# Layer 1 of a hybrid decoder step: output-gate slabs and sample states moved into the slots of the chunk recurrence, with half-width level products, a head norm by logarithm and grouped log gates

## The chip, the cores and the metric

The kernel runs on one core of one Trainium2 chip. The metric is the time of one execution on the device in microseconds; below, "PE" is TensorE's matmul stream, "PEld" its weight loads, "DVE" VectorE, "ACT" ScalarE, "POOL" GpSimd and "SP" the engine that issues most DMAs.

## The reference, cut to what matters

The kernel computes one inference step of two layers for 528 prompt rows and 8 x 4 sample rows. The change concerns only the mixer of layer 1, a gated linear attention with 4 heads (key width 128, value width 256):

```
q, k, v, g, gd = split_cols(h @ w_in, ODD_SIZES)
loga = log_sigmoid(gd @ wgu + bg) / 16                 # one gate per key column and row
for each chunk:                                        # scan, state S (128 x 256 per head)
    b = cumsum(loga)
    o = (q * exp(b)) @ S  +  tril(att(q, k, decay)) @ v
    S = exp(b_last) * S + (k * exp(b_last - b)).T @ v
on = rmsnorm(o, gn) * silu(g)                          # per head; the output gate g
y  = on @ w_out
```

The prompt starts from S = 0 and passes 16 meta rows and then 512 rows; each of the 8 samples starts from a state of its own and has 4 rows. The new states are outputs too.

## The kernel before, in words

Activations lie as [128 partitions of the feature, rows]; there are R = 560 rows, in two halves of 280. Every large product is done to nearly full precision with three matmuls (high x high, low x high, high x low part). A weight matrix is cut into slabs of 256 columns: a DMA brings a slab into one of two slots of RAW, ACT copies its high part (`hi`), POOL subtracts for the low part (`lo`), and PE runs two tiles of 128 columns, each 8 k-steps x 2 halves x 3 matmuls, by the helper `tile_rows` (line 1808). Tile 0 goes to PSUM banks 0 and 1, tile 1 to banks 2 and 3; ACT empties the first and DVE the second. The semaphores are `raw_in`, `hi_done`, `lo_done`, `slab_used`, `acc_done` and `acc_free`.

Each engine has one instruction list in program order, and the order is written out by hand. In layer 1 the stages follow one another so:

- **Projections.** The slabs of q, of the 16 gate columns (`gd`), of k (`ok`, two slabs). Between `gd` and `ok` come the log gates, head by head: two matmuls per half on PE (line 2253), then Abs, Exp and Ln on ACT (lines 1146 to 1150), a min and a subtract on DVE (lines 1624, 1627). Then DVE runs the cumulative sum as four scans (line 1631), and after them empties its tiles of k (line 1616).
- **Levels.** The decayed attention inside a chunk of 64 rows is built from six levels (block sizes 64 to 2) and the diagonal, for two pairs of heads. For each level DVE makes exponents (1656, 1657), ACT exponentiates them, DVE and POOL scale queries and keys (1667, 830), PE makes 18 or 20 products of 64 x 64 (line 2290), and DVE copies the wanted quadrant of each block by a mask into ATT (1677). A product has all 64 query columns although only the later half of each block is kept. The four slabs of v (`ov`) and the first of the four output-gate slabs (`og`) are placed among them.
- **Chunk recurrence.** Rows are padded to 9 prompt chunks of 64 and one of the 32 sample rows. For each chunk PE transposes values and keys (2303, 2306), ACT copies them into VR and KR (1193, 1195), PE makes the state update (2340) and then 16 output products in two parts, from the state (2322) and from ATT (2324), and DVE forms the new state (1745) and moves the outputs into G (1731).
- **Samples.** For each of the 8 samples a DMA brings its state into SIN (512 KB, two buffers), PE makes its state update (2356) and the inter-part of its output (2361: 8 products with the state as weight and 4 moving columns), DVE forms the new state (1585), and a DMA stores it.
- **Head norm.** ACT squares, PE sums over the head's width with a matrix of ones (2373), ACT takes Sqrt (1200), DVE the reciprocal (1764).
- **Gate slabs 1 to 3** of `og` (their loads stand behind the samples in SP's list), Silu on ACT, two multiplies per tile on DVE (1772, 1778), the high and low parts (1226, 1781), and then the four slabs of `out1`, the first of which starts as its k-steps become ready.

Layer 1's feed-forward part and the final norm follow; they are not touched.

Of the kernel before, what the change touches and what calls it, by code (L numbers as in the profile page):

```python
# [23 lines left out]
ALU = mybir.AluOpType  # L24
# [185 lines left out]
def trunk(nc, t, o):  # L210
# [4 lines left out]
    with ExitStack() as ctx:  # L215
# [139 lines left out]
        GATE0 = LK[:, :, :, :].rearrange("p s h n -> p (s h n)")[:, 0:2 * R].rearrange("p (a n) -> p a n", a=2)  # L355
        LE = NRM[:, :, :].rearrange("p a n -> p (a n)")[:, 0:4 * GW].rearrange("p (s h n) -> p s h n", s=2, h=2)
        GSC = NRM[:, 0:2, :]
        GRR = NRM[:, 2:6, :]
        YR, _, _ = region("YR", [RB, 4, 512], F32, 0)
# [68 lines left out]
        WP = NCP * CH  # L428

# [85 lines left out]
        def _(sp):  # L515
# [30 lines left out]
            def load_pair(g, i):  # L546
# [17 lines left out]
                for j in range(2):  # L564
                    sp.wait_ge(lo_done, a + 2 * i + j - 1)
                    sp.dma_start(RAW[:, (a + j) % 2, 0:g.kcs[j], :], srcs[j]).then_inc(raw_in[(a + j) % 2], 16)
# [46 lines left out]
            load_pair(gemms["og"], 0)  # L613

            sgla = t["state_gla"][0]
            for b in range(DB):
# [13 lines left out]
            load_pair(gemms["og"], 1)  # L630
            for name in ("out1", "up1a", "down1a", "up1b", "down1b"):
# [212 lines left out]
        def _(act):  # L844
# [295 lines left out]

            for h in range(GH):
                L = GSC[:, h % 2, :]
                act.wait_ge(la_mm, h + 1)
                if h >= 2:
                    act.wait_ge(la_sub, h - 1)
# [3 lines left out]
                act.wait_ge(la_act, 2 * h + 1)  # L1149
                act.activation(L, L, ACT.Ln, bias=1.0).then_inc(la_act, 1)  # L1150
            odd_rows(gemms["ok"], 4)
# [30 lines left out]
            for j in range(2):  # L1182
                act.wait_ge(*tile_done(og, j, 0, 0))
                act.activation(halved(GATE0[:, j, :]), halves(j), ACT.Silu).then_inc(acc_free[j], 1)
            hi(og.slab0 + 1)

            for c in range(NCH):
                m = CH if c < NCP else NS
                act.wait_ge(vk_tr, c + 1)
                if c >= 2:  # L1190
                    act.wait_ge(o_done, c - 1)
                for par in range(2):
                    act.activation(VR[64 * par:64 * par + m, c % 2, :], PS[0:m, par, :], ACT.Copy)
                for par in range(2):
                    ins = act.activation(KR[64 * par:64 * par + m, c % 2, :], PS[0:m, 2, 2 * GDK * par:2 * GDK * par + 2 * GDK], ACT.Copy)
                ins.then_inc(vk_ev, 1)
# [1262 lines left out]
```

## Time and profile before

| what | value |
|---|---|
| median of 3 runs | 1714.29 us (1706.51 to 1719.15) |
| profiled execution, its own time | 1713.52 us |
| its span, first to last instruction | 1711.7 us |
| mean granted TensorE clock in it | 0.92 of full speed |
| PE busy | 1589.3 us, 93% of the span |
| DVE, ACT, POOL busy | 32%, 31%, 32% |

The rows below come from that one execution; its times count from the start of the span. A merged row of a timeline gives the start, the time from its first start to its last end, the count of instructions (xN), and in brackets how long the engine was idle before it and what ended that. An fp32 matmul stands in the trace as two instructions. "PEclk" is the granted clock, in shares of 2.4 GHz.

### The profile page before, as it was taken

What the parts mean: (1) busy time and instruction counts of PE and PEld (TensorE: products, weight loads), DVE (VectorE), ACT (ScalarE), POOL (GpSimd) and SP (SyncE); (2) the same over time, 40 slices, a digit from 0 to 9 for tenths busy, and PEclk for the clock granted to TensorE, in tenths of its full rate; (3) what the DMA queues carried; (4) which work ended last, traced back from release to release, by engine and by line L of the source; (5) the groups of instructions that cost most, each with busy time, mean ns of one, the idle gap of its engine ahead of it and who ended that gap; (6) DMA issues with size and microseconds to landing.
All of it is one profiled execution on the core that took longest, in us unless ns stands there. A gap on an engine that the chain in (4) does not pass through costs nothing.

```text
span 1711.7 us, 28133 instructions
## 1 busy us (share of the span) xinstructions
PE 1589.3 (93%) x11895; PEld 1479.4 (86%) x11895; DVE 550.5 (32%) x1005; ACT 534.5 (31%) x708; POOL 549.0 (32%) x203
## 2 busy tenths in 40 slices
PE   6888988988999999999888889999989999999996
PEld 5677756578999999999888887788989999999996
DVE  5168785533111101101317762236340111001113
ACT  4233443432433222223353231103333432222231
POOL 4322352022433434333345430002334343434240
PEclk8889996898999999999889897658989999999998
DMA  5531342002222232222222100044212222232221
GB/s 131 174 113 61 125 151 97 1 26 74 74 87 78 74 104 87 85 70 79 64 74 74 51 26 1 1 151 131 76 50 86 86 67 91 87 98 74 71 77 53
DMA packets 117076, 136.12 MB, mean 80 GB/s; under 512 B 5960, under 2 KB 111834, under 8 KB 114945
## 3 DMA queue, kind: packets, MB, share of 16 engines
q1 hardware_dynamic: 113189, 114.04, 21.5%
q0 software_dynamic: 3456, 20.97, 3.5%
q8 instruction: 56, 0.92, 0.2%
q14 instruction: 19, 0.16, 0.0%
q10 hardware_dynamic: 356, 0.03, 0.0%
HBM read 127.14 MB, written 7.94 MB: 79 GB/s over the span
## 4 chain that ended last, share of the span: by engine, by line
PE 87%; DVE 5%; ACT 4%; issue 2%; DMA 1%; POOL 0%; SPq 0%; DVEq 0%; ACTq 0%; POOLq 0%
PE PS L1808 67%; PE PS L2324 2%; PE PS L2361 2%; PE PS L2322 2%; PE PS L2143 1%; PE PS L2356 1%; PE PS L2037 1%; PE PS L2340 1%; PE PS L2290 1%; PE PS L2068 1%; PE PS L2128 1%; PE PS L2106 1%; PE PS L1836 1%; PE PS L2303 1%; PE PS L2025 1%
## 5 line engine op out<-in xcount | busy, mean ns | idle before, releaser
L1808 PE MATMUL PS<-HHI,WHI 128*128 128x280 f32 x2304 | 648.8, 299 | 22.0 <-DVE HLO L1270 10.8
L1808 PE MATMUL PS<-HLO,WHI 128*128 128x280 f32 x2304 | 641.8, 295 | 0.0
L670 POOL TENSOR_TENSOR WLO<-RAW,WHI 128x2048 fp32r<-128x2048 f32 (+2 forms) x89 | 366.1, 4114 | 855.2 <-ACT WHI L868 659.7
L1808 PE MATMUL PS<-HHI,WLO 128*128 128x280 f32 x2304 | 489.9, 295 | 0.0
L1808 PEld LDWEIGHTS PS<-HHI,WHI 128*128 128x128 f32 x2304 | 443.9, 193 | 33.6 <-issue 23.7
L1808 PEld LDWEIGHTS PS<-HLO,WHI 128*128 128x128 f32 x2304 | 443.4, 192 | 0.0
L1808 PEld LDWEIGHTS PS<-HHI,WLO 128*128 128x128 f32 x2304 | 373.2, 192 | 0.0
L868 ACT ACTIVATE WHI<-RAW 128x2048 fp32r<-128x2048 f32 x87 | 166.1, 1909 | 148.7 <-PE PS L1808 146.0
L1808 PE MATMUL PS<-ALO,WHI 128*128 128x280 f32 x704 | 192.8, 291 | 0.0
L1808 PE MATMUL PS<-AHI,WHI 128*128 128x280 f32 x704 | 192.8, 291 | 0.0
L1596 DVE TENSOR_TENSOR AT<-PS,SG 128x560 f32<-128x560 f32 x44 | 32.6, 742 | 473.4 <-PE PS L1808 473.4
L1808 PE MATMUL PS<-AHI,WLO 128*128 128x280 f32 x704 | 147.5, 291 | 0.0
L1569 DVE TENSOR_TENSOR XT<-PS,XT 128x560 f32 x48 | 35.6, 742 | 306.8 <-PE PS L1808 306.8
L1808 PEld LDWEIGHTS PS<-AHI,WHI 128*128 128x128 f32 x704 | 132.5, 188 | 0.0
L1808 PEld LDWEIGHTS PS<-ALO,WHI 128*128 128x128 f32 x704 | 132.3, 188 | 0.0
L1808 PEld LDWEIGHTS PS<-AHI,WLO 128*128 128x128 f32 x704 | 111.7, 188 | 0.0
L664 POOL TENSOR_TENSOR WLO<-RAW,WHI 128x2048 fp32r<-128x2048 f32 x16 | 76.1, 4755 | 99.9 <-ACT WHI L861 93.5
L1117 ACT ACTIVATE AHI<-AT 128x560 f32 x44 | 29.6, 673 | 224.5 <-DVE AT L1596 224.5
L1112 ACT ACTIVATE SG<-PS 128x560 f32<-128x560 f32 x44 | 28.1, 639 | 147.6 <-PE PS L1808 147.2
L893 ACT ACTIVATE NRM<-XT 128x560 f32 (+1 forms) x32 | 21.5, 672 | 135.0 <-DVE XT L1569 134.9
L861 ACT ACTIVATE WHI<-RAW 128x2048 fp32r<-128x2048 f32 x18 | 34.4, 1910 | 20.2 <-PE PS L1808 20.2
L692 POOL TENSOR_TENSOR HLO<-NRM,HHI 128x560 fp32r<-128x560 f32 x16 | 22.7, 1419 | 51.1 <-ACT HHI L886 51.1
(301 smaller groups left out, 1661.9 us busy)
## 6 DMA issues: line engine op xcount, KB each, us to landing
RAW<-in_ffn_w_gate SPq DMA_DIRECT2D x22, 1024.0 KB, 5.3
RAW<-in_ffn_w_up SPq DMA_DIRECT2D x22, 1024.0 KB, 5.3
RAW<-in_ffn_w_down SPq DMA_DIRECT2D x16, 768.0 KB, 4.5
RAW<-in_w_in_odd SPq DMA_DIRECT2D x12, 1024.0 KB, 5.3
RAW<-in_ffn_w_down SPq DMA_DIRECT2D x16, 640.0 KB, 4.3
RAW<-in_w_in_even SPq DMA_DIRECT2D x7, 1024.0 KB, 6.9
RAW<-in_w_out_even SPq DMA_DIRECT2D x4, 1024.0 KB, 5.2
SIN<-in_state_gla SPq DMA_DIRECT2D x8, 512.0 KB, 4.0
```

The lines of the kernel that those rows point to most:

```text
L664: pool.tensor_tensor(WLO[:, s % 2, 0:kc, :], RAW[:, s % 2, 0:kc, :], WHI[:, s % 2, 0:kc, :].bitcast(F32), ALU.subtract).then_inc(lo_done, 1)
L670: pool.tensor_tensor(WLO[:, par, 0:kc, :], RAW[:, par, 0:kc, :], WHI[:, par, 0:kc, :].bitcast(F32), ALU.subtract).then_inc(lo_done, 1)
L861: act.activation(WHI[:, s % 2, :, :], RAW[:, s % 2, :, :], ACT.Copy).then_inc(hi_done, 1)
L868: act.activation(WHI[:, s % 2, :, :], RAW[:, s % 2, :, :], ACT.Copy).then_inc(hi_done, 1)
L1112: act.activation(halved(SG[:, j, :]), halves(j), ACT.Silu).then_inc(acc_free[j], 1)
L1117: act.activation(AHI[:, ds(2 * i + j, 1), :].rearrange("p a n -> p (a n)"), AT[:, j, :], ACT.Copy).then_inc(ahi_ready, 1)
L1569: dve.tensor_tensor(x, halves(j), x, ALU.add).then_inc(acc_free[j], 1)
L1596: dve.tensor_tensor(halved(AT[:, j, :]), halves(j), halved(SG[:, j, :]), ALU.mult).then_inc(acc_free[j], 1)
L1808: ins = pe.matmul(acc[a][:, half, 0:HALF], w[:, slot, k, c0:c0 + P], x[:, k0 + k, HALF * half:HALF * half + HALF], start=first and n == 0 ...
L2322: pe.matmul(out, STATE[:, c % 2, h, 128 * e:128 * e + 128], G[:, h, CH * c:CH * c + m], start=True, stop=False)
L2324: ins = pe.matmul(out, VR[rows, c % 2, x:x + 128], ATT[rows, h // 2, CH * c:CH * c + m], start=not inter, stop=True)
L2361: ins = pe.matmul(PS[:, 7, y:y + DT], SIN[:, b % 2, h, 128 * e:128 * e + 128], G[:, h, WP + DT * b:WP + DT * b + DT], start=True, stop=True)
```

## The change

- **Log gates grouped.** ACT first copies the high part of slab `ok` 1, then does Abs and Exp for all four heads and after that Ln for all four, each head with a buffer of its own (LA). PE puts the first tile of `ok` between heads 1 and 2, and the second after head 3. DVE does the four min operations, then the four subtracts, then the scans.
- **Half-width levels.** The products of the six levels take only the later query half of each block, 32 columns of a chunk; the masked copy moves half as many elements.
- **Recurrence.** The chunk of the sample rows comes first (`CHUNKS`), with buffers of its own (VRS, KRS). The transposes of values and keys are separate steps in banks 2 and 3. The outputs go to banks 4 and 5, state updates of prompt and samples to banks 6 and 7. Gate slabs 1 to 3 are cut into 18 pieces (3, 3 and 2 k-steps of a tile), all in banks 0 and 1, two to a chunk. From the second chunk on, each chunk also does one sample: its update, and its output with the 32 masked query columns as weight (`QM`) and the state's 256 columns as moving operand, the four heads at four output partitions; DVE adds these up in OI, which PE turns back at the end. SP's list has the loads of `og` slabs 2 and 3 and of `out1` slab 0 moved ahead of, or among, the sample states. ACT applies Silu to each gate tile as it ends, into eight buffers in LK and BC.
- **Head norm.** Sqrt and reciprocal become Ln on ACT and Exp with scale -0.5 on ACT; the multiplies and low parts on DVE are interleaved by head; the gate slabs that stood behind the norm are gone from there.

The core of the diff (the buffers' definitions, the semaphore counts of loads and of two unchanged helpers are left out):

```diff
+        CHUNKS = [NCP] + list(range(NCP))
+        GATE_ENDS = [3 * x + 2 for x in range(6)]
@@ sync
+            load_pair(gemms["og"], 1, (0,))
             for b in range(DB):
...
+                if b == 1:
+                    load_pair(gemms["og"], 1, (1,))
+                if b in (4, 6):
+                    load_pair(gemms["out1"], 0, (b // 2 - 2,))
...
-            load_pair(gemms["og"], 1)
@@ scalar
+            hi(ok.slab0 + 1)
             for h in range(GH):
-                L = GSC[:, h % 2, :]
+                L = LA[:, h, :]
...
-                act.wait_ge(la_act, 2 * h + 1)
-                act.activation(L, L, ACT.Ln, bias=1.0).then_inc(la_act, 1)
+            for h in range(GH):
+                act.wait_ge(la_act, h + 1)
+                act.activation(LA[:, h, :], LA[:, h, :], ACT.Ln, bias=1.0).then_inc(la_act, 1)
...
+            for k in range(2):
+                values_out(k)
+                keys_out(k)
+            hi(og.slab0 + 2)
+            for c in range(NCP):
+                if c + 1 < NCP:
+                    values_out(c + 2)
+                gate_out(2 * c)
+                if c + 1 < NCP:
+                    keys_out(c + 2)
+                gate_out(2 * c + 1)
...
-                act.activation(halved(GRR[:, h, :]), ..., ACT.Sqrt, bias=CA[:, C_EPS:C_EPS + 1]).then_inc(ort, 1)
+                act.activation(halved(GRR[:, h, :]), ..., ACT.Ln, bias=CA[:, C_EPS:C_EPS + 1]).then_inc(ort, 1)
+            for h in range(GH):
+                act.wait_ge(ort, h + 1)
+                act.activation(GRR[:, h, :], GRR[:, h, :], ACT.Exp, scale=-0.5).then_inc(orr, 1)
@@ vector
+                ins = dve.copy_predicated(ATT[:, hp, 0:WP].rearrange("p (c b x) -> p c b x", c=NCP, x=size)[:, :, :, half:size],
+                                          late.unsqueeze(1).to_broadcast([P, NCP, CH // size, half]),
+                                          ps[:, 0:WP // 2].rearrange("p (c b x) -> p c b x", c=NCP, x=half))
...
+            for c in range(NCP):
+                if c:
+                    own_keys(c - 1)
+                new_state(c)
+                chunk_out(c)
+                if c:
+                    sample_out(c - 1)        # OI add, then new_states(b)
...
-                dve.reciprocal(GRR[:, h, :], GRR[:, h, :]).then_inc(orr, 1)
...
+                if h:
+                    gated_lo(2 * h - 2)
+                    gated_lo(2 * h - 1)
+            gated_lo(6)
+            gated_lo(7)
@@ tensor
+            for x in range(4):
+                log_gates(x)
+                if x % 2:
+                    one_tile(gemms["ok"], 0, x // 2)
+            for j in range(2):
+                one_tile(gemms["ok"], 1, j)
...
+            def state_update(c):
+                pe.wait_ge(vk_ev, 2 * c + 4)
+                if c:
+                    pe.wait_ge(s_new, GH * c)
+                if c >= 2:
+                    pe.wait_ge(sn_ready, GH * (c - 1))
...
+            def sample_products(b):
+                pe.wait_ge(st_in[b % 2], 16 * (b // 2 + 1))
+                pe.wait_ge(kb_ready, b + 1)
+                pe.wait_ge(s_new, GH * (b + 2))
+                ...                          # 4 updates into banks 6, 7
+                for h in range(GH):
+                    ins = pe.matmul(PS[NS * h:NS * h + NS, 3, 0:GDV], masked_query(h, b), SIN[:, b % 2, h, :], start=True, stop=True)
+                ins.then_inc(oi_done, 1)
...
+            for k in range(2):
+                value_turns(k)
+                key_turns(k)
+            chunk_products(NCP)
             for c in range(NCP):
+                state_update(c)
+                if c + 1 < NCP:
+                    value_turns(c + 2)
+                gate_piece(2 * c)
+                if c + 1 < NCP:
+                    key_turns(c + 2)
+                chunk_products(c)
+                if c:
+                    sample_products(c - 1)
+                gate_piece(2 * c + 1)
...
-            for n in range(1, 4):
-                one_slab(gemms["og"], n)
             slab_loop(gemms["out1"], [(o2lo, k + 1) for k in range(KC)])
```

## Rows read from the trace of the kernel before

**Rows 1.** The page, part 1: busy time, share of the span and instructions of each engine.

```profile
PE 1589.3 (93%) x11895; PEld 1479.4 (86%) x11895; DVE 550.5 (32%) x1005; ACT 534.5 (31%) x708; POOL 549.0 (32%) x203
```

**Rows 2.** Busy time by stretch: length, PE, PEld, DVE, ACT, POOL, PEclk, DMA share, GB/s.

```profile
878.80:921.90 43.10, 35.10 (x208) 31.62 (x208) 21.26 (x15) 24.45 (x26) 10.74 (x3) 0.84 0.24 74
921.90:1019.50 97.60, 87.13 (x1008) 84.85 (x1008) 74.46 (x74) 32.02 (x31) 41.54 (x16) 0.91 0.13 40
1019.50:1115.40 95.90, 91.88 (x464) 72.31 (x464) 21.57 (x55) 20.92 (x41) 4.51 (x1) 0.73 0.01 5
1115.40:1161.40 46.00, 45.89 (x208) 39.17 (x208) 15.70 (x42) 0.00 (x0) 0.00 (x0) 0.50 0.49 156
1161.40:1174.10 12.70, 9.92 (x34) 7.12 (x35) 5.31 (x3) 8.27 (x12) 0.00 (x0) 0.83 0.72 224
1174.10:1211.10 37.00, 37.00 (x288) 36.77 (x287) 24.33 (x18) 10.63 (x10) 14.40 (x3) 1.00 0.27 86
1211.10:1227.80 16.70, 14.12 (x96) 13.95 (x97) 7.39 (x13) 6.92 (x10) 4.61 (x1) 0.90 0.20 64
```

**Rows 3.** PE's timeline through chunk 1.

```profile
1027.74 1.13 PE L2340 MATMUL PS<-VR,KR 64*128 64x256 f32 x8 [0.97 <-ACT KR L1195]
...
1028.81 1.06 PE L2303 MATMUL PS<-CA,G 128*64 128x128 f32 x8
...
1030.14 0.33 PE L2322 MATMUL PS<-G,STATE 128*128 128x64 f32 x2
...
1035.50 0.48 PE L2340 MATMUL PS<-VR,KR 64*128 64x256 f32 x1
```

**Rows 4.** Busy time in chunk 1 and in a later chunk; columns as in rows 2.

```profile
1027.74:1035.50 7.76, 7.76 (x51) 6.37 (x52) 1.66 (x4) 1.93 (x4) 0.00 (x0) 1.00 0.00 0
1067.64:1081.72 14.08, 14.08 (x55) 11.05 (x55) 2.41 (x6) 1.93 (x4) 0.00 (x0) 0.50 0.00 0
```

**Rows 5.** The chain that ended last: start, us, what; recurrence, samples, norm.

```profile
1067.64 2.03 PE PS L2340 x8
...
1081.72 2.03 PE PS L2340 x8
...
1115.44 1.92 PE PS L2324 x16
1117.36 1.87 PE PS L2356 x8
...
1169.88 4.22 PE PS L2373 x16
```

**Rows 6.** Groups of ACT's instructions from 879 to 900 us: count, busy, mean ns.

```profile
L1148 ACT ACT_TABLE_LOAD x4 | 5.1, 1283 | 0.1
...
L1148 ACT ACTIVATE NRM<-NRM 128x560 f32<-128x560 f32 x4 | 2.7, 670 | 0.0
...
L868 ACT ACTIVATE WHI<-RAW 128x2048 fp32r<-128x2048 f32 x1 | 1.9, 1901 | 0.0
```

**Rows 7.** DVE's scans (minimum, median, longest ns), and its timeline after them.

```profile
L1631 DVE TENSOR_TENSOR_SCAN BC<-CG,BC x4: 1392/3564/5723, 899.9 to 912.5; 128x608 f32<-128x608 f32 x4
...
913.84 0.71 DVE L1616 TENSOR_SCALAR G<-PS 128x560 f32<-128x560 f32 x1
```

**Rows 8.** POOL's timeline around the scans.

```profile
901.03 4.65 POOL L670 TENSOR_TENSOR WLO<-RAW,WHI 128x2048 fp32r<-128x2048 f32 x1 [21.78 <-ACT WHI L868]
905.64 5.68 POOL L664 TENSOR_TENSOR WLO<-RAW,WHI 128x2048 fp32r<-128x2048 f32 x1
```

**Rows 9.** Groups by shape in the levels' stretch, from 919 to 1020 us.

```profile
L2290 PE MATMUL PS<-LQ,LK 128*64 128x64 f32 x432 | 16.4, 239 | 9.7 <-DVE LQ L1667 9.7
...
L1677 DVE COPY_PREDICATED ATT<-CG,PS 128x576 f32<-128x576 int32 x14 | 11.5, 821 | 17.0 <-PE PS L2290 16.8
```

**Rows 10.** The group of DVE's new sample states, four to a sample.

```profile
L1585 DVE SCALAR_TENSOR_TENSOR SNEW<-SIN,EB,PS 128x256 f32<-128x256 f32 x32 | 13.2, 476 | 26.6 <-PE PS L2356 26.6
```

**Rows 11.** The group of DVE's low parts behind the gates.

```profile
L1781 DVE TENSOR_TENSOR HLO<-G,HHI 128x560 fp32r<-128x560 f32 x8 | 5.3, 734 | 0.0
```

More of the change, by code:

```diff
@@ L563, in load_pair @@
                     srcs = [w[:, :, ds(c0 + 512 * i, 256)], w[:, :, ds(c0 + 512 * i + 256, 256)]]
-                for j in range(2):
+                for j in which:
                     sp.wait_ge(lo_done, a + 2 * i + j - 1)
@@ L629, in _ @@
             store(o["new_gla_prompt"][0, 0].rearrange("h d e -> d h e"), STATE[:, NCP % 2, :, :])
[L630 to L631 removed]
+            load_pair(gemms["out1"], 1)
+            for name in ("up1a", "down1a", "up1b", "down1b"):
                 load_all(gemms[name])
@@ L1183, in _, with values_out @@
                 act.wait_ge(*tile_done(og, j, 0, 0))
-                act.activation(halved(GATE0[:, j, :]), halves(j), ACT.Silu).then_inc(acc_free[j], 1)
+                act.activation(halved(gate(j)), halves(j), ACT.Silu).then_inc(acc_free[j], 1)
             hi(og.slab0 + 1)
-            for c in range(NCH):
+            def values_out(k):
+                c = CHUNKS[k]
                 m = CH if c < NCP else NS
[L1189 to L1196, printed above, removed]
+                act.wait_ge(vk_tr, 2 * k + 1)
+                if 2 <= c < NCP:
+                    act.wait_ge(o_done, c)
+                dst = VR[:, c % 2, :] if c < NCP else VRS
+                act.activation(dst[0:m, :], PS[0:m, 2, :], ACT.Copy)
+                act.activation(dst[64:64 + m, :], PS[0:m, 3, :], ACT.Copy).then_inc(vk_ev, 1)
@@ new lines, in keys_out, with gate_out @@
+            def keys_out(k):
+                c = CHUNKS[k]
+                m = CH if c < NCP else NS
+                act.wait_ge(vk_tr, 2 * k + 2)
+                dst = KR[:, c % 2, :] if c < NCP else KRS
+                act.activation(dst[0:m, :], PS[0:m, 2, 0:2 * GDK], ACT.Copy)
+                act.activation(dst[64:64 + m, :], PS[0:m, 2, 2 * GDK:4 * GDK], ACT.Copy).then_inc(vk_ev, 1)
+            def gate_out(piece):
+                if piece not in GATE_ENDS:
+                    return
+                x = GATE_ENDS.index(piece)
+                n, j = 1 + x // 2, x % 2
+                act.wait_ge(*tile_done(og, j, n, n))
+                act.activation(halved(gate(2 * n + j)), halves(0), ACT.Silu).then_inc(acc_free[j], 1)
+                if j and n < 3:
+                    hi(og.slab0 + n + 2)
@@ L2248, in _, with log_gates @@
             pe.wait_ge(ht_ready, KC * (norm_no["mix1"] + 1))
-            for h in range(GH):
+            def log_gates(h):
                 if h >= 2:
@@ L2364, in _ @@
+            pe.wait_ge(oi_ev, DB)
+            for e in range(2):
+                ins = pe.transpose(PS[:, 3, P * e:P * e + P], OI[:, P * e:P * e + P], ident(P))
+            ins.then_inc(oi_done, 1)
+            pe.wait_ge(s_new, GH * NCP)
+            pe.wait_ge(o_ev, NCH)
             pe.wait_ge(in_gla, 32)
@@ L2374, in _ @@
                     ins.then_inc(osq_used, 1)
-            for n in range(1, 4):
-                one_slab(gemms["og"], n)
             slab_loop(gemms["out1"], [(o2lo, k + 1) for k in range(KC)])
```

209 lines of the change are left out of this document (124 added, 85 removed).

## The prediction

> **What bounds the kernel now.** I read the page first, then busy time by stretch, then PE's own timeline inside the stretches that the change rebuilds. PE is busy for 93% of the span and the other three engines for about 32% each [rows 1]; so the question for every microsecond is whether PE does less, gets a higher clock, or stops waiting. The stretches [rows 2] answer it differently. In the log gates PE works 35.1 of 43.1 us: there is idle time. In the levels it works 87.1 of 97.6. In the recurrence (95.9 us), and still more in the samples (46.0 us, PE 45.9), PE is hardly ever idle, but its granted clock is 0.73 and 0.50. The three gate slabs (37.0 us) run at 1.00. So moving the gate slabs into the recurrence fills no holes: there are none. What it can win is cheaper sample products, clock, and the waits around the stretches.
>
> That the recurrence is slow by its clock is seen in two chunks. Chunk 1 takes 1035.50 - 1027.74 = 7.76 us at clock 1.00: update 1.07, twelve transposes 1.33, output products 5.36 (differences of starts) [rows 3, 4]. A later one takes 14.08 us at 0.50, its update 2.03 [rows 4, 5]. Chunks 1 to 8 together, from 1027.74 to 1115.44, take 87.7 us, 10.96 each: 3.2 us a chunk are lost to the clock.
>
> **Log gates.** Before, ACT loads a table ahead of every Exp and every Ln, 8 times 1.28 us (the four of one line are shown [rows 6]), and the scans start at 899.9. A scan takes 1.39 us undisturbed and up to 5.72 [rows 7]; the long ones lie beside POOL's two low parts, 901.0 to 911.3 [rows 8]. Only at 913.84 does DVE empty the k tile for which PE stands. After: six loads fewer (7.7 us), but heads 2 and 3 wait for PE's first k tile (37.0 / 6 = 6.2 us [rows 2]), so the subtracts end near 896, about 4 us earlier. The copy of slab `ok` 1 now stands ahead of the gates on ACT (1.9 us [rows 6], of which 0.6 delays the chain), so POOL's first low part comes before the scans and one is left beside them. Four scans: 4 x 1.4 plus one block of 4.6 gives 906.5, the evacuation 907.2, against 914.5: 7 us. If both blocks stay: 4; if none: 11. I take **-7**.
>
> **Levels.** The trace shows no 32-column product. The 432 records of 64 columns take 16.4 us of merged busy time [rows 9]. If the weight load sets the pace, half the columns bring nothing; if the columns do, 8 us. The masked copy (0.82 us; 12 of 14 halved) moves half the elements: at most 0.4 us each, 5 in all, but DVE lies on PE's path only where PE waits for it, 9.7 us in all [rows 9]. I take 2 + 2 = **-4**, between 0 and -11.
>
> **Recurrence with samples and gate pieces.** The old cost is 95.9 + 46.0 + 37.0 = 178.9 us [rows 2]. The new one, first at full clock:
> - Up to the end of chunk 0. Before, from 1019.5 to 1027.74 [rows 2, 3], 8.2 us: two sets of transposes with ACT's copies between them, an update, chunk 0's products. After: a third set, between 1.3 (transposes alone) and 4.1 (half of the 8.2), 2.5 taken; the sample chunk's products, 1.92 at half clock [rows 5], 1.0; two gate pieces, 2 x 37.0 / 18 = 4.1. Sum 15.8.
> - Chunks 1 to 8: 7.76 + 4.1 + one sample. The sample's update is the old one, 1.87 us at half clock [rows 5], about 1.0 at full. Its output product is new: eight instructions of 256 columns. One after the other, at the 0.264 us of a 280-column fp32 instruction (4.22 / 16 [rows 5]), they take 1.9; if the four heads, which fall on different output partitions, run fully side by side, 0.5. The levels' products, which lie on two partition halves, are the nearest: 16.4 / 432 = 0.04 us each [rows 9], where 64 of 280 columns at 0.264 would be 0.06, so they do overlap; I take 0.8. So 13.7 a chunk; eight make 109.6, less 1.3 because the last has no transposes: 108.3.
> - New waits on PE: `state_update` waits for the new sample states (`sn_ready`), since both use banks 6 and 7. Behind it stand the next transposes, a piece and all products, and ACT waits for those. DVE needs 4 x 0.476 [rows 10] and an add, some 2.3 us, after the sample's product; the piece between covers 2.3 us when it has 3 k-steps and 1.5 when it has 2. In all 2.5 us. `key_turns` waits for ACT's copy of values; all copies of a chunk are 1.93 us [rows 4], and a piece covers that share of it. Without that cover it would cost up to 1.9 a chunk.
> - Clock: I keep the 3.2 us a chunk of before, 25.6 in all. The output products, in which the clock was lost, are unchanged and now followed by a sample, which loses it too; the pieces bring it back, as `og` 1 to 3 hold 1.00, but each must first run part of itself slow. The bounds are 0 and the all-slow case below.
>
> Sum: 15.8 + 108.3 + 2.5 + 25.6 = 152.2, against 178.9: **-26.7**.
>
> Moved DMAs: SP issues the third gate slab ahead of the first sample state, the fourth after sample 0, and `out1` slab 0 among samples 3 to 6. Each is needed a chunk or more (some 17 us) after its issue, and the DMA share is 0.01 in the recurrence and 0.49 in the samples [rows 2], so I cost them at nothing; sample states are loaded two chunks ahead. POOL's low parts of four slabs now fall into the recurrence. The slowed scans show what one does to a DVE instruction beside it: up to 4.3 us [rows 7, 8]. DVE's steps in a chunk (2.41 us before [rows 4]) are done one chunk before PE needs them, so I take no loss; where one is hit with no cover, it costs those 4.3.
>
> **Tail.** Before, the norm stretch (12.7) and the start of `out1` (16.7) make 29.4 us [rows 2]; the reciprocals and most multiplies lay under the gate slabs. That cover is gone. After: turning OI and adding it, 1.2 (estimate); squares, sums and Ln in place of Sqrt as before, 12.5; Exp's table and one Exp, 1.28 + 0.67 [rows 6]; then 16 multiplies and 8 low parts on DVE at 5.3 / 8 = 0.66 us [rows 11], 15.9, with `out1`'s first slab behind them; PE ends some 4.2 later, its last three k-steps at 1.5. Sum 35.8: **+6.4**, from +4 to +11 (POOL's next low part can block one of DVE's).
>
> Total -7 - 4 - 26.7 + 6.4 = -31.3. The profiled execution took 1713.5 us, 0.8 below the median; that gives 1682, and I predict **1683 us** for the median.
>
> **A rule against the rows.** In the samples PE is busy 45.9 of 46.0 us, and its granted clock is 0.50 [rows 2]; a busy row doesn't bring the higher level here. The Trainium skill (TensorE: Matmul & The Clock Gate, Part 1: The HAM clock gate) tells it otherwise: a busy PE gets the full clock, and only an idle one falls back. By that rule the new recurrence, which has almost no idle time, would lose nothing, and the sum would be 1657; by the rows it is 1683. This trace disagrees with the rule as far as small products go.
>
> **Rivals.**
> - *Full clock.* The pieces, 18 wide matmuls or 12 each and twice a chunk, hold the clock at 1.00 through the products. Then the 25.6 us go: 1657. For it: chunk 1, soon after a gate slab, ran at 1.00 throughout [rows 4]. Against: the later chunk stayed at 0.50 although its update and transposes came between two sets of products. The rule above is this case. 0.15.
> - *Hand-overs.* The order is one chain now, PE to ACT to PE and PE to DVE to PE in each chunk, and one slab copy on ACT (1.9 us) or low part on POOL shifts it. With 2.2 us of waits a chunk instead of 0.3, and a blocked low part in the tail: 1683 + 15 + 5 = 1703. For it: banks 2, 3, 6 and 7 each change hands between prompt and sample work in every chunk. Against: in the old recurrence, with such a chain too, PE is busy 91.9 of 95.9 us [rows 2]. 0.22.
> - *Slower: the clock stays at half through the whole recurrence.* Then a chunk costs 14.08 + 7.8 (pieces, at the ratio 14.08 / 7.76 or a little more) + 3.5 (sample) = 25.4 instead of 13.7 + 3.2: 68 us more in eight, 1751. It decides from a loss of 7.1 us a chunk, where the whole gain is gone (9.2 for over 1% slower). For it: the samples never came back from 0.50. Against: in the old recurrence transposes and updates alone, 2.4 us of a chunk, brought the mean to 0.73. 0.07.
> - *The change doesn't do what it says in the small parts:* half-width products bring 0 and grouped gates 4 us: 1690, inside the forecast.
>
> **How the numbers follow.** My forecast, with a clock loss between 2 and 4.5 us a chunk and the bounds above, reaches from 1671 to 1696 and has 0.56. The range for 8 in 10 takes in much of the full-clock case and of the hand-overs: 1660 to 1704. A change under 1% (17 us; the three runs spread over 0.7%) can't well be told from none. Faster by more than that, below 1697: the forecast, full clock, and a third of the hand-overs, 0.78. Same: the rest of the hand-overs, 0.15. Slower: 0.07.
>
> **What would show it.** The changed kernel's profile should show: the k tile emptied near 907; the first chunk transposes near 1008; a recurrence of about 150 us with PE nearly always busy, a mean clock near 0.8, and output products at two speeds; sample outputs of 0.5 to 1 us at full clock; no stretch of gate slabs alone; and about 35 us from the last piece to `out1`'s second slab, in which DVE is the engine that ends last. The prediction is wrong if pieces don't lift the clock, if PE waits for ACT or DVE over 1 us in each chunk, or if a sample's output product takes 2 us at full clock (+9).

## The result and the profile after

The changed kernel takes **1693.11 us** (median of 4 runs, 1682.15 to 1694.29); the kernel before took 1713.60 beside it (4 runs). The ratio is 0.9891, 95% interval 0.9858 to 0.9925: about 1% faster. The forecast was 1683, with a range of 1660 to 1704. The direction and the mechanism held; two thirds of the gain arrived. The profiled execution took 1691.95 us, its span is 1690.4.

A whole execution is a poor ruler here, since the part ahead of the log gates, whose code is the same in all kernels, itself takes 869 to 881 us in the profiled executions. So I compare **one stretch**: from the first log-gate product to the start of `out1`'s second slab. Ahead of that stretch and behind it nothing is changed. PE's timeline of the kernel before gives its two ends, and the end of the log gates (the first matmul of the first `ov` slab) between them:

```profile
879.46 2.15 PE L2253 MATMUL PS<-GD,WGU 16*128 16x280 f32 x8 [0.71 <-ACT GD L1139]
...
921.93 0.36 PE L1808 MATMUL PS<-HHI,WHI 128*128 128x280 f32 x1 [0.88 <-issue]
...
1227.80 0.37 PE L1808 MATMUL PS<-HHI,WHI 128*128 128x280 f32 x1 [0.27 <-DVE XT L1569]
```

That is 348.3 us before. After, it is 1205.43 - 877.83 = 327.6: **20.7 us less**, where the forecast was 31.3. Part 1 of the page after, which answers to [rows 1]:

```profile
PE 1564.5 (93%) x11833; PEld 1453.1 (86%) x11833; DVE 530.1 (31%) x1014; ACT 528.9 (31%) x706; POOL 546.3 (32%) x203
```

Busy time by stretch after, columns as in [rows 2]: the log gates, the levels, the start of the recurrence up to the end of chunk 0, chunks 1 to 8, the norm, and `out1`'s first slab.

```profile
877.83:915.75 37.92, 34.21 (x209) 32.28 (x209) 17.00 (x15) 15.78 (x19) 9.53 (x2) 0.86 0.27 84
915.75:1014.08 98.33, 87.90 (x1008) 85.96 (x1009) 74.67 (x79) 32.02 (x31) 40.52 (x16) 0.90 0.16 51
1014.08:1033.80 19.72, 15.86 (x112) 12.92 (x112) 2.92 (x9) 9.22 (x14) 9.04 (x2) 0.83 0.06 21
1033.80:1169.80 136.00, 136.00 (x785) 109.23 (x785) 37.00 (x95) 19.74 (x35) 9.07 (x2) 0.79 0.24 74
1169.80:1182.40 12.60, 9.01 (x35) 5.88 (x33) 0.42 (x1) 9.65 (x15) 0.00 (x0) 0.95 0.52 166
1182.40:1205.43 23.03, 14.44 (x96) 14.27 (x97) 17.66 (x28) 10.71 (x14) 4.62 (x1) 0.78 0.00 1
```

Against [rows 2]: in chunks 1 to 8 PE is busy in all of 136.00 us, at clock 0.79; the levels take as long as before (98.3, 97.6); in the last stretch DVE is the busiest engine, as foreseen.

One chunk of the recurrence in PE's timeline shows how that clock comes about:

```profile
1068.92 1.13 PE L2460 MATMUL PS<-VR,KR 64*128 64x256 f32 x8
...
1073.20 0.60 PE L2428 MATMUL PS<-CA,G 128*64 128x128 f32 x4
1073.64 0.33 PE L2445 MATMUL PS<-G,STATE 128*128 128x64 f32 x2
1073.90 0.43 PE L2447 MATMUL PS<-ATT,VR 64*128 64x64 f32 x2
...
1079.08 0.69 PE L2447 MATMUL PS<-ATT,VR 64*128 64x64 f32 x2
1079.69 2.08 PE L2470 MATMUL PS<-NRM,KB 32*128 32x256 f32 x8
1081.70 1.08 PE L2477 MATMUL PS<-SIN,NRM 128*32 128x256 f32 x8
1082.71 0.60 PE L1898 MATMUL PS<-HHI,WHI 128*128 128x280 f32 x1
...
1085.67 0.29 PE L1898 MATMUL PS<-HHI,WHI 128*128 128x280 f32 x1
```

The update takes 1.13 us (full clock), and so it goes on until near the end of the output products, whose pairs grow from 0.43 to 0.69 us. The sample's update then takes 2.08 and its output 1.08, where e1 below has 1.13 and 0.64 at full clock, and the next piece begins slow and is fast again only from 1085.67 on. None of these chunks waits for anything, and they have some 7 us each at half clock (here 1078.6 to 1085.7).

### The profile page after: what moved, and what is told of

It reads as the page before. It is cut to its first block, busy times and chain, and to the rows that moved or that the text cites. A ratio compares the mean times of both kernels' runs of the same rounds, so it can differ in the third digit from the quotient of the medians.

```text
span 1690.4 us, 28001 instructions
## 1 busy us (share of the span) xinstructions
PE 1564.5 (93%) x11833; PEld 1453.1 (86%) x11833; DVE 530.1 (31%) x1014; ACT 528.9 (31%) x706; POOL 546.3 (32%) x203
## 4 chain that ended last, share of the span: by engine, by line
PE 87%; DVE 5%; ACT 4%; issue 2%; DMA 1%; POOL 0%; SPq 0%; DVEq 0%; ACTq 0%; POOLq 0%
PE PS L1898 69%; PE PS L2447 2%; PE PS L2445 1%; PE PS L2233 1%; PE PS L2470 1%; PE PS L2127 1%; PE PS L2400 1%; PE PS L2218 1%; PE PS L2158 1%; PE PS L2196 1%; PE PS L1926 1%; DMA CA<-in_consts_a 1%; PE PS L2115 1%; PE PS L1978 1%; PE PS L2040 1%
## 5 line engine op out<-in xcount | busy, mean ns | idle before, releaser
L1898 PE MATMUL PS<-HHI,WHI 128*128 128x280 f32 x2304 | 657.5, 302 | 28.4 <-DVE HLO L1319 10.8
L1898 PEld LDWEIGHTS PS<-HHI,WHI 128*128 128x128 f32 x2304 | 449.8, 195 | 46.9 <-issue 37.0
L1898 PEld LDWEIGHTS PS<-HLO,WHI 128*128 128x128 f32 x2304 | 449.3, 195 | 0.0
L1898 PEld LDWEIGHTS PS<-HHI,WLO 128*128 128x128 f32 x2304 | 377.4, 194 | 0.0
L1618 DVE TENSOR_TENSOR XT<-PS,XT 128x560 f32 x48 | 35.6, 741 | 301.7 <-PE PS L1898 301.7
```

Source lines behind the costliest of these rows:

```text
L1618: dve.tensor_tensor(x, halves(j), x, ALU.add).then_inc(acc_free[j], 1)
L1898: ins = pe.matmul(acc[a][:, half, 0:HALF], w[:, slot, k, c0:c0 + P], x[:, k0 + k, HALF * half:HALF * half + HALF], start=first and n == 0 ...
```

## The experiments

Each kernel is the changed kernel with the edit named. The table splits the stretch; "start" runs from the first value transposes to the end of chunk 0, "chunks" from there to the turning of OI, "tail" to `out1`'s second slab. All but the last column are differences of starts in PE's timeline of the profiled execution, in us. (Before: 140.0 for gates and levels, 178.9 for recurrence, samples and gate slabs, 29.4 for the tail.)

| kernel | gates, levels | start | chunks | tail | sum | median of the runs |
|---|---|---|---|---|---|---|
| before | 140.0 | 178.9 | (in start) | 29.4 | 348.3 | 1712.8 to 1714.1 |
| changed | 136.3 | 19.7 | 136.0 | 35.6 | 327.6 | 1693.1 (4) |
| e1_split | 136.2 | 20.0 | 126.6 | 37.4 | 320.2 | 1680.8 (4) |
| e9_split_again | 136.2 | 20.1 | 126.6 | 37.4 | 320.3 | 1684.7 (1) |
| e2_lo_after_scans | 132.9 | 20.2 | 136.0 | 35.7 | 324.8 | 1688.1 (4) |
| e3_wide | 133.5 | 21.7 | 138.0 | 35.4 | 328.6 | 1693.2 (1) |
| e4_pieces_after | 136.1 | 16.0 | 198.0 (with all pieces) | 35.4 | 385.6 | 1745.2 (4) |
| e5_four | 136.2 | 20.0 | 138.7 | 37.0 | 331.9 | 1693.3 (4) |
| e11_four_again | 136.2 | 20.0 | 138.7 | 37.0 | 331.9 | 1689.6 (1) |
| e6_roots | 136.3 | 19.7 | 136.0 | 42.2 | 334.2 | 1697.4 (1) |
| e7_three | 128.5 | 22.0 | 133.1 | 35.6 | 319.2 | 1684.4 (4) |
| e8_four_best | 130.2 | 21.9 | 132.9 | 36.8 | 321.8 | 1678.9 (4) |
| e10_start | 136.2 | 19.9 | 136.0 | 35.6 | 327.7 | 1683.4 (1) |
| e12_best | 129.7 | 18.7 | 128.7 | 35.6 | 312.7 | 1682.0 (4) |

The sum repeats: two traces of one kernel agree within 0.1 us (e1 and e9, e5 and e11), while the whole times of single executions differ by up to 10 us. e10 shows where from: it is 8.5 us faster than the profiled execution of the changed kernel, and its stretch is as long. It came to the log gates 7.7 us earlier, through code that is the same. A slice of layer 0, first of the changed kernel,

```profile
300.00:350.00 50.00, 45.95 (x353) 29.43 (x352) 26.05 (x45) 22.82 (x59) 0.00 (x0) 0.89 0.00 1
```

then of e10:

```profile
300.00:350.00 50.00, 43.35 (x385) 29.53 (x383) 26.03 (x46) 22.98 (x59) 0.00 (x0) 1.00 0.00 1
```

The granted clock (third number from the end) is 0.89 in the one and 1.00 in the other.

### What the pieces do: none, three and four a chunk

**e4_pieces_after**: no pieces in the chunks, all 18 behind them; the load of `out1`'s second slab stands behind the sample states, since its buffer comes free later. (Of the edit, PE's part is shown; SP's load and ACT's copies out of the gate tiles move with it.)

```diff
             for c in range(NCP):
                 state_update(c)
...
-                gate_piece(2 * c)
...
-                gate_piece(2 * c + 1)
+            for x in range(18):
+                gate_piece(x)
```

> The changed kernel with all 18 gate pieces moved behind the recurrence, the samples left in it. Theory A (the pieces fill no idle time of the old recurrence, but now cover the waits for ACT's copies and DVE's sample states and bring the clock back once a chunk): a chunk takes 15 to 17 us instead of 17.0 although it lost 4.1 us of work, PE waits 2 to 4 us in each, and the pieces then take 37 us: 15 to 30 us slower than the changed kernel, near the kernel before. Theory B (the pieces' place is worth nothing, all of the gain is the cheaper samples): a chunk takes 12.9 us, and the time is within 4 us of the changed kernel.

1745.2 us, ratio to the kernel before 1.0191 (1.0172 to 1.021): 52 us slower than the changed kernel (58.0 by the stretch) and slower than before. Theory A had the direction, and about half of the size. Two chunks in its windows, and PE's waits in the recurrence (line, what it waited for, us in all, times, longest):

```profile
1041.99:1063.04 21.05, 17.57 (x68) 12.45 (x69) 4.66 (x13) 1.94 (x4) 0.00 (x0) 0.50 0.32 100
1063.04:1084.10 21.06, 17.57 (x69) 12.46 (x69) 4.66 (x13) 1.94 (x4) 0.00 (x0) 0.50 0.17 51
```

```profile
PE PS L2461 <- DVE SNEW L1634: 15.4, 7, 2.2
PE PS L2429 <- ACT VR L1222: 11.5, 9, 1.3
```

These two chunks without their pieces take 21.05 us each, more than the 17.0 with them: they are at half clock throughout, though PE is busy for 17.6 of it, and wait for the sample states (2.2) and ACT's copies (1.3). Chunks 5 and 6 take as long; chunks 4 and 7 take 19.3 at a clock of 0.59. So the pieces pay twice: with them the clock is higher, and they are the cover for the two new waits that I had costed at 2.5 us in all. It isn't the new idle time alone that keeps the clock low: the later chunk of [rows 4] was at 0.50 with PE busy in all of its 14.08 us.

**e1_split**: three pieces a chunk, the third between the output products of heads 1 and 2; the same k-steps in all.

```diff
+                    if h == 2 and c < NCP:
+                        gate_piece(3 * c + 1)
...
-                ks = ((0, 1, 2), (3, 4, 5), (6, 7))[part]
+                ks = ((0, 1), (2, 3), (4, 5), (6, 7), (0, 1), (2, 3), (4, 5), (6,), (7,))[part]
```

> The changed kernel with three gate pieces in a chunk in place of two (2 k-steps each, some of 1), the second in the middle of the output products. Theory A (the clock falls because products and sample make one stretch of some 9 us without wide matmuls, and the 3.3 us a chunk are the price of each such stretch): the granted clock of the recurrence rises from 0.79 to 0.95 or more, a chunk takes 14 instead of 17.0 us, and the kernel is some 20 to 25 us faster than the changed one (about 1670). Theory B (the loss follows the mean share of narrow work in a chunk, wherever the pieces stand): clock 0.79 as before, chunks of 17 us, within 3 us of the changed kernel. Theory C (smaller pieces open the waits that the larger ones covered): clock up, but chunks of 16 us or more with PE waiting on ACT or DVE over 1 us in each.

1680.8 us, ratio 0.9812 (0.9794 to 0.983). The start, the chunks and the tail in its windows, and a sample's two steps in its chunk 2:

```profile
1006.60:1026.63 20.03, 16.17 (x113) 13.02 (x113) 2.92 (x9) 9.22 (x14) 9.05 (x2) 0.83 0.06 20
1026.63:1153.18 126.55, 124.37 (x785) 102.30 (x785) 35.77 (x93) 19.97 (x35) 9.10 (x2) 0.88 0.25 80
1153.18:1190.61 37.43, 25.18 (x133) 21.77 (x131) 19.24 (x33) 20.35 (x28) 4.61 (x1) 0.82 0.18 57
```

```profile
1054.63 1.13 PE L2472 MATMUL PS<-NRM,KB 32*128 32x256 f32 x8
1055.69 0.64 PE L2479 MATMUL PS<-SIN,NRM 128*32 128x256 f32 x8
```

The clock rises to 0.88 and the chunks lose 9.4 us, although 2.2 us of waits (for sample states) are new in them; start and tail take 2.1 more. That lies between theories A (0.95) and B (0.79). So how the wide work is cut and where it stands matters, not only how much there is.

**e5_four**: four pieces a chunk, most of a single k-step, and the sample's products between heads 1 and 2. On DVE the sample's results are taken ahead of the chunk's outputs, which the cut below leaves out.

```diff
+                    if h == 2 and c < NCP:
+                        gate_piece(4 * c + 1)
+                        if c:
+                            sample_products(c - 1)
+                    if h == 3 and c < NCP:
+                        gate_piece(4 * c + 2)
...
+                ks = ((0, 1), (2,), (3,), (4,), (5, 6), (7,), (0,), (1,), (2, 3), (4, 5), (6,), (7,))[part]
```

> The changed kernel with four gate pieces a chunk instead of two (same k-steps in all, 2/1/1/1 or 2/2/1/1), spread so that no run of narrow products is longer than some 3 us at full clock, and with the sample's products between the output products of heads 1 and 2. Theory A (the clock is lost where narrow products follow one another for long without a wide piece; the split into three brought 0.79 to 0.88): clock of 0.95 or more, 14 to 14.5 us a chunk, 1668 to 1674 us. Theory B (only the share of wide work in a chunk counts, and three pieces had already reached what that gives; a piece of one k-step is too short to lift the clock): clock near 0.88 and 1681 us as with three. Theory C (the finer order turns into waits on DVE's states and outputs): PE waits of more than 1 us a chunk, 1690 or more.

1693.3 us: all that three pieces brought is gone, and none of the three theories fits: the clock of the chunks is 0.79, and PE is busy in 138.66 of their 138.67 us. Chunks 1 and 4 in its windows; both have the same instructions, with the same pieces of 2, 1, 1 and 1 k-steps:

```profile
1029.55:1048.72 19.17, 19.17 (x100) 15.15 (x99) 4.80 (x13) 2.46 (x5) 0.00 (x0) 0.69 0.26 79
1085.85:1099.86 14.01, 14.01 (x100) 11.46 (x99) 4.65 (x13) 2.46 (x5) 0.00 (x0) 1.00 0.25 76
```

No waits in either, and 19.2 us at clock 0.69 against 14.0 at 1.00. Shorter narrow runs don't hold the clock by themselves.

**e9_split_again, e11_four_again**: second traces of e1 and e5, unchanged, to see whether that is chance.

> The kernel with three pieces a chunk once more, unchanged, for a second trace. If its higher clock comes from the number of pieces, chunks 1 to 8 again have a clock of 0.87 to 0.89 and the chunks take the same times in the same order (17.6, 14.4, 15.9, 17.8, 16.1, 18.0, 15.1 us). If it comes from where the chunks happen to fall against the throttle's decisions, the order of long and short chunks is another one, and the clock lies somewhere between 0.80 and 0.90.

> The kernel with four pieces a chunk once more, unchanged. Its first trace had chunks from 14.0 to 21.0 us with the same instructions. By the number of pieces: the same order again. By where the chunks fall: another order, with a sum that may differ by 5 us or more.

It isn't. e1's chunks 1 to 7 took 17.56, 14.35, 15.93, 17.75, 16.10, 18.02, 15.12 us; e9's, which came 9.8 us later, took 17.58, 14.32, 15.93, 17.76, 16.18, 17.96, 15.11. The same chunks of e11:

```profile
1028.27:1047.46 19.19, 19.19 (x99) 15.17 (x98) 4.80 (x13) 2.46 (x5) 0.00 (x0) 0.69 0.26 80
1084.58:1098.61 14.03, 14.03 (x100) 11.47 (x99) 4.66 (x13) 2.46 (x5) 0.00 (x0) 1.00 0.27 76
```

So in both pairs of executions the clock's course came back with the program, chunk by chunk. A chunk's own work doesn't set it: e1's chunks 2 and 5 have the same pieces and take 14.35 and 16.10 us. And the chunks 5 to 7 of e7 below (14.33, 15.94 and 17.75 us) take the times of e1's chunks 2 to 4, whose pieces are the same. What sets the course, these runs don't tell.

### The log gates

**e2_lo_after_scans**: ACT holds back the high part of the first slab of v (`ov` 0) until three scans are done, so that POOL's low part starts behind them. (The expectation of e7 calls it slab `ok` 1; the line that waits makes the v slab's.)

```diff
+                    act.wait_ge(b_ready, GH - 1)
```

> The changed kernel with one added wait: ACT makes the high part of the first v slab only when three of the four scans are done, so that POOL's low part can't lie beside them. Theory A (a scan is slow only because POOL's low part blocks it): all four scans take 1.4 us, the k tile is emptied 4.3 us earlier against the start of the log gates, PE's last k tile takes 6.3 instead of 8.0 us because PE idles less before it, and the first v slab starts 5 to 6 us earlier. Theory B (the later low part makes the first v slab late): the v slab starts at the same time or later, PE waiting for POOL.

1688.1 us, ratio 0.9841 (0.9823 to 0.986). In the changed kernel, DVE's and POOL's timelines:

```profile
893.89 2.70 DVE L1677 TENSOR_TENSOR BC<-BC,NRM 128x560 f32<-128x560 f32 x4 [1.95 <-ACT NRM L1171]
896.50 9.71 DVE L1681 TENSOR_TENSOR_SCAN BC<-CG,BC 128x608 f32<-128x608 f32 x4
906.13 0.71 DVE L1664 TENSOR_SCALAR G<-PS 128x560 f32<-128x560 f32 x1
...
899.98 4.95 POOL L684 TENSOR_TENSOR WLO<-RAW,WHI 128x2048 fp32r<-128x2048 f32 x1 [15.74 <-ACT WHI L881]
```

In e2:

```profile
899.50 5.37 DVE L1682 TENSOR_TENSOR_SCAN BC<-CG,BC 128x608 f32<-128x608 f32 x4
904.78 0.72 DVE L1665 TENSOR_SCALAR G<-PS 128x560 f32<-128x560 f32 x1
...
905.58 4.60 POOL L684 TENSOR_TENSOR WLO<-RAW,WHI 128x2048 fp32r<-128x2048 f32 x1 [18.37 <-ACT WHI L881]
```

Four scans take 9.71 us with the low part beside them and 5.37 without: it stalled one scan by 4.3. The Trainium skill (SBUF — State Buffer, SBUF: two separate sides) calls the port pair that VectorE and GpSimd share an exclusive lock, held for the whole instruction by whichever comes first, when the VectorE operation has two SBUF inputs and the GpSimd one reads SBUF; these rows, with a scan of two inputs, agree. Theory A held, a little under its size: the log gates went from 37.92 to 914.08 - 880.81 = 33.27 us, where it had 5 to 6 us less; levels and start gave 1.8 of the 4.65 back.

### Half width

**e3_wide**: the level products at 64 columns again; the masked copy still moves only half, now out of the full-width products (its edit is left out).

```diff
-                            q = q.rearrange("p (b x) -> p b x", x=size)[:, :, size // 2:size]
-                            ps = PS[64 * par:64 * par + m, bank, CH // 2 * c:...]
+                            ps = PS[64 * par:64 * par + m, bank + c // 8, CH * (c % 8):CH * (c % 8) + m]
```

> The changed kernel with full-width level products again (64 columns) and the half-size masked copies kept, so that PE's part alone is undone. Theory A (the products go at the pace of their weight loads, and half the columns only make PE look idler): groups of 36 products take 1.20 to 1.22 us as with half width, and the stretch from the first v slab to the end of the first gate slab is 96 to 97 us, up to 1.5 shorter than the 97.5 of the changed kernel, because products and the slabs behind them run at a higher granted clock. Theory B (columns cost): groups take longer than 1.20 us and the stretch grows by 2 us or more.

Groups by shape in the levels of the changed kernel, which answer to [rows 9],

```profile
L2400 PE MATMUL PS<-LQ,LK 128*64 128x32 f32 x432 | 16.8, 240 | 9.6 <-DVE LQ L1717 9.6
...
L1738 DVE COPY_PREDICATED ATT<-CG,PS 128x288 f32<-128x288 int32 x12 | 7.0, 587 | 18.7 <-PE PS L2400 18.6
```

and of e3:

```profile
L2398 PE MATMUL PS<-LQ,LK 128*64 128x64 f32 x432 | 16.1, 237 | 10.2 <-DVE LQ L1717 10.2
```

32 columns take 16.8 us for the 432 records, 64 take 16.1 here and 16.4 before: half the columns bring nothing. Nor is it the spread of the kept columns: at full clock the records of one level (size 64, one run of 32 columns) start 29.1 ns apart with 32 columns and 29.9 with 64, and in the next level, with two runs of 16, 28.5 apart with either. The shorter copy is real (587 ns, 821 before), but PE's wait in the levels is for the scaled queries (LQ), not for the copies, and stays at 10 us; DVE waits for PE 18.7 us ahead of the copies, 17.0 before. Worse, the narrower products come with a lower clock: from the log gates to the levels' end it is 0.89 with 32 columns and 0.92 with 64, and that part is 2.7 us shorter with 64. The levels alone take 1012.38 - 916.81 = 95.6 us at 0.95 in e3, 98.3 at 0.90 in the changed kernel. The start and the chunks give 4.0 back, so the sum is 1 us longer: where clock is won in one stage, the next begins with another clock.

### The start and the norm

**e10_start**: ACT copies the high part of the second gate slab (1.9 us) behind the sample chunk's values and keys, not ahead of them.

```diff
-            hi(og.slab0 + 1)
...
             for k in range(2):
                 values_out(k)
                 keys_out(k)
+                if k == 0:
+                    hi(og.slab0 + 1)
```

> The changed kernel with ScalarE's copy of the second gate slab's high part (1.9 us) moved behind the first values and keys that it copies for the recurrence. The start of the recurrence was 4 us above the forecast, with four waits on ScalarE's copies in it (1.7, 0.85, 1.3 us and 0.8 in front). If they are the cause, the first wait of 1.7 us is gone, and the time from the first value transposes to the end of chunk 0 falls from 19.7 to some 18 us. Rival: the next copy waits for the slab copy instead and the stretch stays within 0.5 us of 19.7.

The rival held: 19.90 us instead of 19.72. PE's waits in the start of the changed kernel,

```profile
PE PS L2428 <- ACT NRM L1221: 1.7, 1, 1.7
PE PS L2428 <- ACT VR L1221: 1.3, 1, 1.3
```

and of e10:

```profile
PE PS L2429 <- ACT VR L1220: 2.0, 1, 2.0
PE PS L2429 <- ACT NRM L1220: 1.3, 1, 1.3
```

The wait moved from the sample chunk's values (NRM) to chunk 0's (VR). ACT is one list, and the slab copy delays whichever copy comes behind it.

But the waits are not why the start was longer than forecast. The kernel before has 8.24 - 5.13 = 3.1 us of them ahead of its chunk 1, and the forecast was built on that stretch; its first update runs at full clock, while the changed kernel's takes nearly twice as long. The start and the update of the kernel before, and the update of the changed kernel:

```profile
1019.50:1027.74 8.24, 5.13 (x48) 4.17 (x49) 2.17 (x6) 5.46 (x9) 4.51 (x1) 1.00 0.15 49
...
1023.11 1.14 PE L2340 MATMUL PS<-VR,KR 64*128 64x256 f32 x8 [2.09 <-ACT KR L1195]
```

```profile
1023.41 2.08 PE L2460 MATMUL PS<-VR,KR 64*128 64x256 f32 x8
```

**e6_roots**: Sqrt on ACT and reciprocals on DVE as before the change.

```diff
-                act.activation(halved(GRR[:, h, :]), ..., ACT.Ln, ...).then_inc(ort, 1)
+                act.activation(halved(GRR[:, h, :]), ..., ACT.Sqrt, ...).then_inc(ort, 1)
...
+                dve.reciprocal(GRR[:, h, :], GRR[:, h, :]).then_inc(orr, 1)
```

> The changed kernel with ScalarE's Sqrt and VectorE's reciprocals put back in the head norm; all else as changed. If the reciprocals (3.6 us each in the trace before, four of them) now stand on the path, since no gate slabs lie behind the norm any more, the first multiply starts some 2 to 3 us later, the engine that sets the tail gets 14 us more work and saves 4 exponentials elsewhere, and the time from the last piece to the second slab of out1 grows from 35.4 to some 46 us: 1703. Rival: the reciprocals lie beside other waits of the tail (VectorE was busy only 17.7 of 23 us there), and the tail grows by 5 us or less: under 1698.

The tail is 42.2 us instead of 35.6: 6.6 more, between the two expectations. DVE's timeline has it:

```profile
1177.44 14.19 DVE L1854 RECIPROCAL NRM<-NRM 128x560 f32<-128x560 f32 x4 [5.81 <-ACT NRM L1257]
1191.55 1.41 DVE L1860 SCALAR_TENSOR_TENSOR G<-G,COLS,NRM 128x560 f32<-128x560 f32 x2
```

The four reciprocals start behind the first root and end 14.2 us later, and the first multiply waits for the last of them, as all four stand ahead of it in DVE's list. So the logarithm is worth 6.6 us against reciprocals in this order, now that no gate slabs stand behind the norm; reciprocals placed head by head among the multiplies were not run.

### Together

**e7_three** is e1, e2 and e3 in one kernel; **e8_four_best** is e5, e2 and e3; **e12_best** is e7 with the edit of e10.

> The changed kernel with three pieces a chunk, the low part of slab ok 1 held back until three scans are done, and full-width level products with the narrow copy kept: the three single edits together, which brought 12, 5 and some 1 to 3 us. If they add up, as they lie in different stages: 1673 to 1675 us. If a gain in one stage is given back in the next one (a clock that starts lower, a load that comes late), 1678 or more.

> As the kernel with three edits together, but with four pieces a chunk. By theory A (length of the narrow stretches) 1662 to 1667 us; by theory B (share of wide work) the same as with three pieces, 1673 to 1675; by theory C (new waits) 1682 or more.

> Three pieces a chunk, the late low part, full-width level products and the moved slab copy together. Adding up what each gave alone in its own stage (9, 3 to 4, 3 and 2 us, of 1693) gives 1674 to 1677. If the recurrence gives part of it back by another clock, as it did with the first three together (1684), 1680 to 1685.

Stage by stage they don't add up. e7 wins 7.7 us in gates and levels, but its start has 22.0 us and its chunks 133.1, where e1 alone has 20.0 and 126.6: 8.4 are given back, all in the clock (0.82 in the chunks, 0.88 in e1). In the sum this nearly cancels: the single edits' -7.4, -2.8 and +1.0 give 318.4, and e7 has 319.2. e8 goes the other way: its chunks take 132.9 us where e5 alone has 138.7, and its sum is 8.3 below the 330.1 of its single edits. And with e10's edit, worth nothing alone, e12 is another 6.5 us below e7, though PE still waits 4.1 us in its start; the clock is higher (0.91 in the start and 0.86 in the chunks, against 0.69 and 0.82 in e7):

```profile
869.03:998.76 129.73, 118.38 (x1216) 113.78 (x1217) 87.36 (x93) 47.67 (x48) 49.74 (x18) 0.92 0.21 63
998.76:1017.45 18.69, 14.62 (x112) 11.73 (x113) 2.92 (x9) 9.49 (x14) 9.05 (x2) 0.91 0.06 21
1017.45:1146.14 128.69, 126.79 (x786) 103.78 (x786) 36.47 (x94) 19.97 (x35) 9.08 (x2) 0.86 0.25 78
1146.14:1181.73 35.59, 23.41 (x132) 20.05 (x130) 18.64 (x31) 20.37 (x28) 4.61 (x1) 0.84 0.19 60
```

By the stretch e12 is the best, 312.7 us: 14.9 under the changed kernel and 35.6 under the one before. Its median, 1682.0 (ratio 0.984, 0.9779 to 0.9902), doesn't show it, as its four runs spread from 1667 to 1689. That it, e1 (0.9812) and e8 (0.9829) beat the kernel before is clear from their intervals; which of the three is fastest over many runs is not. Against the expectations, by the medians: e7 (1684.4) and e12 (1682.0) came out as the cases in which gains are given back, e8 (1678.9) between its theories.

## Why the prediction came out as it did

- **What binds (right).** The gain is in the recurrence and comes from cheaper sample products and the clock, not from filled holes. A sample takes 1082.71 - 1079.69 = 3.02 us where it took 46.0 / 8 = 5.75 [rows 2], both at half clock; that is 22 us in eight. What the pieces do for the clock and the waits, e4 shows.
- **The chunks (right in the sum, in part by luck).** Forecast for chunks 1 to 8: 108.3 + 2.5 of waits + 25.6 lost to the clock = 136.4. Measured: 136.0. Two misses cancel: the waits were nothing, covered by the pieces; the clock, with a chunk that is a little dearer at full clock than my 13.7 (e5's chunk 4 took 14.0 at 1.00), cost 2.1 more. The loss of 3.2 us a chunk was carried over from the old chunks, and with the same work cut otherwise e1's chunks take 126.6 us and e5's 138.7; so a forecast within 0.4 us is luck. The moved DMAs and POOL's low parts cost nothing, since PE is busy in every microsecond of it. A sample's output products take 0.64 us at full clock (e5, e1) and 1.08 at half; I had 0.8.
- **The start (the step that was mis-sized).** 15.8 forecast, 19.7 measured. The waits were sized right: the forecast holds 8.24 - 5.13 = 3.1 us of them from the start of before and 2.5 - 1.3 = 1.2 in the third set of transposes, 4.3 in all, and 19.72 - 15.86 = 3.9 are measured. What failed is PE's work: 15.8 - 4.3 = 11.5 us, all at full clock, against 15.9 at a mean clock of 0.83. By that clock some 3.4 us of it are lost (an estimate, 0.17 of 19.7), and the two pieces here have 3 k-steps each, 4.6 us and not 4.1. I had costed the clock for chunks 1 to 8 and left it out of the start, which had 1.00 before. So recurrence, samples and pieces brought 23.2, not 26.7.
- **The levels (mis-sized, and of the other sign).** -4 forecast, +0.7 measured. I named the case that the columns don't set the pace and then took a quarter of the gain of the other one, 2 of 8 us; e3 shows nothing gained, and clock lost. The 2 us of the copies came only in e3, where the levels take 95.6 us against 97.6 before, and not by the way that I gave: PE's 9.7 us of waiting [rows 9] are put down to LQ, the scaled queries, and stay (10.2 in e3); the clock is higher (0.95 against 0.91). I divided a wait among DVE's work at large that the row gives to one tile.
- **The log gates (mis-sized).** -7 forecast, -4.5 measured. The scans were right, one blocked (9.71 us; I had 10.2). Heads 2 and 3 came later than I had it: counted from the first log-gate product, the k tile is empty 1.3 us later than forecast. And the last k tile takes 915.75 - 906.90 = 8.85 us, where the one before took 7.33 (914.60 to 921.93): PE had stood idle 2.83 us ahead of it (0.88 before), and it ran at 0.81 instead of 1.00. In e2, without the blocked scan, this loss is gone too. I had costed no clock in this term.
- **The tail (right).** +6.4 forecast, 35.6 - 29.4 = +6.2 measured; DVE's multiplies and low parts end it, in 1200.59 - 1184.38 = 16.2 us (15.9 forecast).

The terms that missed: 4.7 (levels) + 3.5 (recurrence, all of it in the start) + 2.5 (gates) = 10.7; the tail came 0.2 better than forecast. Forecast and stretch lie 31.3 - 20.7 = 10.6 us apart, the same but for rounding.

**The rivals.** *Full clock* is out: 0.79. It was the rule of the Trainium skill (TensorE: Matmul & The Clock Gate, Part 1) that a busy PE gets the full clock; in chunks 1 to 8 PE is busy in 136.00 of 136.00 us, and yet the clock falls to half within the output products of all but the last, so this trace disagrees with it for products of 64 columns. *Hand-overs* are found in the start (3.9 us, where the forecast had 4.3) and nowhere in the chunks. *Slower* was a real danger: e4 shows a chunk at 0.50 throughout, 21.05 us before its pieces are counted, and that kernel is slower than before. *The small parts do nothing*, put at 1690, is nearest to the median, and it is half true: the products' half width brought nothing, the gates little over their lower bound; the rest of the miss is the start.

**What stays open.** Why the clock in a chunk is what it is. It is no chance (e9, e11), it isn't the length of the narrow runs alone (e5), nor the number of pieces (e7 against e1), and an edit in the stages ahead changes it (e3, e7, e12). That the course comes back is shown by two executions each of two kernels, and no more.

## What to carry to other kernels

Where one engine is always busy and its clock is what gives, wide work put among narrow work can pay by the clock and as cover for the waits beside it; but what a way of cutting it brings must be measured in the whole kernel (three pieces a chunk took 9.4 us off the chunks, four added 2.7), since a gain in one stage can change the clock in the next. When a stretch is longer than forecast, split both the forecast and the measurement into waits and work before blaming the waits that the profile lists: in the start here the forecast already held them. Half as many columns is not half the time: look for a pair of rows that shows whether columns or instructions set the pace, and ask of every wait which tile it is for before crediting it with a faster step. To judge edits of a few microseconds, compare the stretch that they touch between two unmoved instructions; in two pairs of executions it repeated within 0.1 us, where whole executions spread by 10 to 20.

## What was not expected of the hardware

- A matmul of 128 x 64 weights takes the same time with 32 moving columns as with 64 (240 and 237 ns, 16.8 and 16.1 us for 432), and with the narrower one the granted clock was lower (0.90 in the levels of the changed kernel, 0.95 in e3's).
- The granted clock's course came back with the program: seven chunks of 14.3 to 18.0 us had the same times within 0.08 us each in a second execution that arrived 9.8 us later, while layer 0, with code that is the same in all kernels, had 0.89 in one execution and 1.00 in another between 300 and 350 us.
